# A two-layer decoder trunk with routed experts: three kept weight chunks instead of one, a ring of eight instead of twelve, and VectorE's waits for itself moved

## What is computed

```python
def peer_ffn(h, w_q, sub_keys, expert_u, expert_v):      # per block of 128 rows
    q = jnp.einsum('nd,de->ne', xb, w_q).reshape(n, 8, 2, 128)
    s = jnp.einsum('nhie,ike->nhik', q, keys)
    top_s, top_i = lax.top_k(s, 16)                      # per head and half
    cand_s = top_s[:, :, 0, :, None] + top_s[:, :, 1, None, :]
    best_s, best_pos = lax.top_k(cand_s.reshape(n, 8, 256), 16)
    idx = ...                                            # 8 heads x 16 experts of 16384
    gate = jax.nn.softmax(best_s, axis=-1)
    act = jax.nn.gelu(jnp.einsum('nhkd,nd->nhk', expert_u[idx], xb))
    return jnp.einsum('nhk,nhkd->nd', gate * act, expert_v[idx])
```

## Time and profile before

| | before |
|---|---|
| median of 3 runs | 1624.89 us (1624.58 to 1625.01) |
| the profiled execution, its own time | 1618.27 us |
| its span | 1616.2 us |
| TensorE matmul busy | 1189.6 us, 74% of the span |
| VectorE busy | 1149.4 us, 71% |
| ScalarE busy | 651.6 us, 40% |
| DMA moved | 665.08 MB |

### The profile page before, as it was taken

The page is one execution under the profiler, slowest core; times in us unless marked ns, Lnnn a source line. Parts: engine busy times, 40 slices in busy tenths (PEclk is TensorE's granted clock), DMA queues, the critical chain, the costliest instruction groups (busy, mean ns, idle before and its releaser), DMA issues.

```text
span 1616.2 us, 22343 instructions
## 1 busy us (share of the span) xinstructions
PE 1189.6 (74%) x7488; PEld 589.1 (36%) x7488; DVE 1149.4 (71%) x3098; ACT 651.6 (40%) x1743; POOL 600.5 (37%) x542
## 2 busy tenths in 40 slices
PE   8977776777649986968786788789697955555546
PEld 3662232234316662422263356444234611111111
DVE  4498768568687687776677867779855876666654
ACT  0233255233336664653233466556322333333332
POOL 1036334434324343324333424432342344444441
PEclk9999998989879998989898899899898978777787
DMA  9899999999999999999999999999999999999995
GB/s 373 352 368 418 422 422 421 422 422 421 423 421 421 423 420 422 421 423 422 423 422 422 396 424 424 420 422 419 402 425 422 419 422 421 421 421 421 420 420 236
DMA packets 84371, 665.08 MB, mean 412 GB/s; under 512 B 9408, under 2 KB 9680, under 8 KB 11424
## 3 DMA queue, kind: packets, MB, share of 16 engines
q0 software_dynamic: 74752, 540.13, 80.7%
q1 hardware_dynamic: 9504, 123.53, 18.2%
HBM read 662.57 MB, written 1.05 MB: 411 GB/s over the span
## 4 chain that ended last, share of the span: by engine, by line
DMA 37%; PE 29%; DVE 21%; issue 6%; ACT 5%; POOL 1%; POOLq 0%; ACTq 0%; DVEq 0%; SPq 0%
DMA ring<-in_experts,idx 36%; PE acc L947 12%; DVE ring L1614 7%; PE act_bank L621 7%; PE dve_bank L607 5%; PE act_bank L854 2%; DVE onehot L1245 2%; POOL ring L511 1%; ACT diag L1175 1%; DVE scratch L1245 1%; PE act_bank L607 1%; ACT h L1086 1%; DVE h L1409 1%; DVE picked L1571 1%; ACT scratch L1006 1%
## 5 line engine op out<-in xcount | busy, mean ns | idle before, releaser
L511 POOL DMA_INDIRECT ring<-in_experts,idx x510 | 573.5, 1125 | 936.5 <-PE acc L947 742.3
L1614 DVE CUSTOM_DVE_ANT_0 ring<-ring,hn 128x1024 f32<-128x1024 f32 x512 | 625.9, 1235 | 322.4 <-DMA ring<-in_experts,idx 309.6
L947 PE MATMUL acc<-ring,diag 64*64 64x512 f32 x4080 | 598.5, 711 | 327.8 <-ACT diag L1175 303.1
L947 PEld LDWEIGHTS acc<-ring,diag 64*64 64x64 f32 x4080 | 153.8, 152 | 677.6 <-ACT diag L1175 427.7
L1006 ACT ACTIVATE acts<-dots 128x2 f32<-128x2 f32 x256 | 52.1, 204 | 764.2 <-DVE dots L1614 763.5
L621 PE MATMUL act_bank<-hnT,wbuf 128*128 128x128 f32 x1728 | 221.1, 287 | 25.5 <-ACT h L1086 20.5
L621 PEld LDWEIGHTS act_bank<-hnT,wbuf 128*128 128x128 f32 x1728 | 208.2, 199 | 71.3 <-issue 62.9
L1006 ACT ACT_TABLE_LOAD x148 | 189.9, 1283 | 13.0 <-DVEq L367 2.2
L1175 ACT ACTIVATE diag<-cst,coefs 128x64 f32<-128x64 f32 x512 | 150.2, 340 | 10.2 <-PE acc L947 1.9
L1166 ACT ACTIVATE coefs<-acts,gate 128x1 f32<-128x1 f32 x512 | 122.8, 286 | 12.1 <-ACT scratch L1006 0.8
L1006 ACT ACTIVATE scratch<-act_bank 128x512 f32<-128x512 f32 (+3 forms) x73 | 35.7, 489 | 73.5 <-PE act_bank L621 62.9
(11 more groups left out here) (173 smaller groups left out, 996.2 us busy)
## 6 DMA issues: line engine op xcount, KB each, us to landing
wbuf<-in_weights SPq DMA_DIRECT2D x48, 2048.0 KB, 12.4
ring<-in_weights SPq DMA_DIRECT2D x7, 2048.0 KB, 20.2
ring<-in_experts,idx POOLq DMA_INDIRECT x510, 22.5
kept<-in_weights SPq DMA_DIRECT2D x2, 2048.0 KB, 22.2
wbuf<-in_weights SPq DMA_DIRECT2D x2, 512.0 KB, 6.3
wbuf<-in_weights SPq DMA_DIRECT2D x1, 1024.0 KB, 8.7
scratch<-in_bias POOLq DMA_DIRECT2D x1, 1024.0 KB, 11.9
scratch<-in_bands POOLq DMA_DIRECT2D x1, 768.0 KB, 13.5
```

The lines of the kernel that those rows point to most:

```text
L511: pool.indirect_dma_start(ring[:, n % RING], None, io[f"experts{layer}"], bass.IndirectOffsetOnAxis(idx[:, at:at + 1], 0),).then_inc(sem(f ...
L947: last[rows] = pe.matmul(acc[rows][half][home:home + HALF_P], diag[part, n % DIAGS], ring[part, slot, D + half * CW:D + (half + 1) * CW], ...
L1614: dve.tensor_tensor_reduce(out=ring[:, slot, 0:D], in0=ring[:, slot, 0:D], in1=hn[:, phase % NBLK], scale=1.0, scalar=0.0, op0=ALU.mult, o ...
```

## The change

Five things are altered. RING goes from 12 to 8. KEPT goes from one to three chunks per layer: chunks 7, 8 and 9 of layer 0, chunks 13, 15 and 11 of layer 1; the two query chunks 8 and 9 of the first block no longer lie in the ring, and STAGED_AT places five chunks in four. ASKED_FIRST goes from 2 to 10, and the top-16 searches of heads 6 and 7 of the first block from slots 4 and 5 to slots 8 and 12. VectorE's lane gets `run`, which starts an instruction and leaves its wait `pending` until the next instruction of the lane; a dot between the two is started without it. `copy_even` lets its copies themselves raise `even_copied`.

```diff
-RING = 12
+RING = 8
-STAGED_AT = (5, 3, 0, 1, 2, 4, 5)
+STAGED_AT = (3, 2, 0, 1, 3)
-KEPT = ((7,), (13,))
+KEPT = ((7, 8, 9), (13, 15, 11))
-ASKED_FIRST, QUERIED_BY = 2, 14
+ASKED_FIRST, QUERIED_BY = 10, 14
-TOPS_DUE = [-3, -2, 0, 1, 2, 3, 4, 5]
+TOPS_DUE = [-3, -2, 0, 1, 2, 3, 8, 12]
...
+            def settle(self):
+
+                if self.pending:
+                    self.after(self.pending)
+                    self.pending = None
+
+            def run(self, operation, *operands, name=None, **more):
+
+                self.settle()
+                self.pending = self.start(operation(*operands, **more), name)
...
             def tt(out, in0, in1, op=ALU.mult, name=None):
-                lane(dve.tensor_tensor(out, in0, in1, op), name)
+                lane.run(dve.tensor_tensor, out, in0, in1, op, name=name)
...
-                lane.after(started[-1])
+                lane.pending = started[-1]
...
             def copy_even(phase):
 
+                lane.settle()
                 for rows in range(2):
                     dve.wait_ge(sem(f"pairs_summed{rows}"), (phase + 1) * STEPS * GROUPS + AHEAD)
...
-                        started = lane.start(dve.tensor_copy(h[part, phase % NBLK, cols], acc[rows][half][part]))
-                    lane.after(started)
-                    lane.tell("even_copied")
+                        started = lane.start(dve.tensor_copy(h[part, phase % NBLK, cols], acc[rows][half][part]),
+                                             "even_copied" if rows else None)
+                    lane.pending = started
```

More of the change, by code:

```diff
@@ L350, in __init__ @@
             def __init__(self, eng, own):
-                self.eng, self.own, self.count, self.seen = eng, own, {}, {}
+                self.eng, self.own, self.count, self.seen, self.pending = eng, own, {}, {}, None
             def start(self, instruction, name=None):
@@ L1270, in square_sum @@
             def square_sum(b, out):
-                lane(dve.tensor_tensor_reduce(out=out, in0=h[:, b], in1=h[:, b], scale=1.0, scalar=0.0,
-                                              op0=ALU.mult, op1=ALU.add, accum_out=stat[:, 0:1]))
+                lane.run(dve.tensor_tensor_reduce, out=out, in0=h[:, b], in1=h[:, b], scale=1.0, scalar=0.0,
+                                              op0=ALU.mult, op1=ALU.add, accum_out=stat[:, 0:1])
             def row_root():
@@ L1339, in bias_scores @@
                     top = stat[:, 64:64 + n]
-                    lane(dve.reduce_max(top, part, AX))
+                    lane.run(dve.reduce_max, top, part, AX)
                     tt(part, part, top.unsqueeze(2).to_broadcast([P, n, keys]), ALU.subtract, "scores_biased")
@@ L1357, in mixer0 @@
                     part = probs[:, i % 2].rearrange("p (j k) -> p j k", k=keys)
-                    lane(dve.reduce_sum(total, part, AX))
-                    lane(dve.reciprocal(total, total))
+                    lane.run(dve.reduce_sum, total, part, AX)
+                    lane.run(dve.reciprocal, total, total)
                     tt(part, part, total.unsqueeze(2).to_broadcast([P, n, keys]), name="probs_ready")
@@ L1558, in expert_numbers @@
                     lane.after(started[1])
-                    lane(dve.tensor_copy(place, pos_lo[:, picks]))
+                    lane.run(dve.tensor_copy, place, pos_lo[:, picks])
                     stt(beyond, row, float(WHOLE), place, ALU.is_ge, ALU.mult)
+                    lane.settle()
                     lane.start(dve.tensor_tensor(row, row, beyond, ALU.add))
@@ L1650, in last_rows @@
                     home = slice(half * HALF_P, (half + 1) * HALF_P)
-                    lane(dve.tensor_copy(h[0:HALF_P, NBLK - 1, half * CW:(half + 1) * CW], acc[0][half][home]))
+                    lane.run(dve.tensor_copy, h[0:HALF_P, NBLK - 1, half * CW:(half + 1) * CW], acc[0][half][home])
+                    lane.settle()
                     lane.tell("last_rows_ready0")
@@ L1657, in experts @@
                     g = first + n // BODY
+                    if n == 0:
+                        lane.settle()
                     dot(phase, g, n % BODY)
```

47 lines of the change are left out of this document (30 added, 17 removed).

## The result

| | before | after |
|---|---|---|
| median | 1624.91 us, 4 runs (1624.58 to 1625.01) | 1648.86 us, 4 runs (1640.79 to 1655.09) |
| ratio | | 1.0145 (1.01 to 1.019) |
| the profiled execution, its own time | 1618.27 us | 1640.79 us |
| its span | 1616.2 us | 1639.0 us |
| DMA moved | 665.08 MB | 656.69 MB |

The change is slower by 1.45%, 24 us, where 5 us less was forecast; the time lies far outside 1609 to 1630. In two later series it was slower by 1.17% and 1.26% (e8, e13). The runs of the changed kernel lie 14 us apart, those of the kernel before 0.4.

What follows compares the result with a forecast made beforehand. DMA was taken to bound the kernel. Bytes -19.9, standstills +19.1, VectorE's waits -4.4 and the start +0.2 gave -5.0 us, from 1624.89 to 1619.9 us, range 1609 to 1630.

Steps and rivals of the forecast that it cites:

- Bytes: Four second-block chunk loads (8, 9 of layer 0; 11, 15 of layer 1) go: -19.9 us, nothing hidden.
- nor around the other removed loads: Outside the fifth place, no removed load has a room (gather m's landing minus issue of m + 4) short.
- the fifth place: Mixer 1, gather 340: short by 1.6 us plus 5.0 for the spared load issued at 1126.85, 6.6 in all.
- five places: Bursts at gathers 62, 142, 192, 268, 340 with rooms under 5.7 us: standstills 2.7, 4.4, 2.2, 3.2, 6.6, sum +19.1.
- a standstill shifts everything behind it, so that only the largest of a burst counts: Within one burst of side work neighbours' shortfalls do not add; only the largest is priced.
- m = 192: Gather 192, in one burst of side work: room 3.5 us against 5.7 needed, short by 2.2.
- VectorE's waits: 203 dots no longer wait for VectorE itself, about 0.1 us each; in the bursts -4.4 us (nothing to -6.6).
- first rival: The moved waits are worth nothing, as the skill page says: +0.6 us, 1625.5 us, no change; chance 20%.
- The start: First sums and gathers 8 to 16, moved heads answering the shallow ring: +0.2 us (3 less to 4 more).
- From there I let them land every 2.5 us: After gather 12 lands at 121.2 us, landings every 2.5 us put gather 16 at 131.2, against 131.0 before.
- second rival: Each standstill slows the next two sums (1.2 GHz clock): 3.5 us per place, +12.4, 1637; chance 22%, at about 1629.
- Its milder form: Standing still slows one sum at each of the five places: +3.7 us in all, 1628.6 us.

Runs made afterwards that it cites:

- e8: The changed kernel itself run again on another chip, nothing altered; ratio to the kernel before 1.0117.
- e13: The changed kernel again, as baseline on one chip with e14 and e16; 1644.51 us, ratio to the kernel before 1.0126.
- e5: The kernel before (12 slots) with the four second-block chunk loads cut to 64 KB each, leaving stale weights; ratio to the kernel before 0.9894.
- e14: The changed kernel with only layer 0's chunks 8 and 9 spared, layer 1's 11 and 15 loaded again; 1649.83 us, ratio to before 1.015.
- e4: The changed kernel with all four spared chunks loaded again for the second blocks (bytes of before, 8 slots); ratio to the kernel before 1.0195.
- e16: The same kernel as e4, run on the chip of e13; 1654.53 us, ratio to the kernel before 1.018.
- e7: The changed kernel with 10 slots, the loads of before and heads 6 and 7 ahead as before; ratio to the kernel before 1.0022.
- e1: The kernel before (12 slots, one kept chunk, old head order) with only VectorE's waits moved; ratio to the kernel before 0.9991.
- e2: The changed kernel with VectorE's waits as they were before; ratio to the kernel before 1.0161.
- e3: The changed kernel with heads 6 and 7 ahead of the first sums as before; ratio to the kernel before 1.0165.
- e11: The changed kernel with 10 slots and two kept chunks per layer, waits and heads moved; ratio to the kernel before 0.9926.
- e17: The same kernel as e11, run again beside e18 on one chip; 1612.42 us, ratio to the kernel before 0.9923.
- e9: The kernel before, 12 slots and its bytes kept, gathers issued only 8 slots ahead of the sums; ratio to the kernel before 1.0222.
- e18: The kernel of e17 with heads 6 and 7 ahead of the first sums as before; 1618.76 us, ratio to the kernel before 0.996.

## Why the prediction was wrong, step by step

**The bound was right.** DMA is it, and e5 shows that with 12 slots bytes are time: 17 us for 19.

**Bytes: counted in full, half came back.** The step that failed is "nor around the other removed loads". There I took the rooms from the trace of before as they were, with the loads still in the queues. But a load that goes takes its 5.0 us away from every gather behind it, as I had reckoned at the fifth place alone. Ahead of gather 122 one load is missing; what is behind could land 5.0 us earlier, the sums were not ready for it, and DMA stood still there for 3.4 to 4.6 (changed kernel, e8, e13, e14; nothing in e4 and e16). The fifth place itself came out about as reckoned: its dips, gathers 335 to 349, lose 0.7 us in e4, which has the load, and 5.8 in the changed kernel and in e8 (6.6 forecast). The two places together are nearly all that was lost of the saving. Measured for all four loads: 10.0 us left of 19.9 (e13 to e16), where I had 14.9.

**Rooms: five places at 19.1 us, measured 37 to 42.** With the bytes of before, the ring of 8 with moved waits and heads costs 32 us (e4); by my terms it would be 14.1 (the list without the 5.0 of the spared load) + 0.2 - 4.4 = 9.9. Two steps failed. The first: "a standstill shifts everything behind it, so that only the largest of a burst counts". The view of DMA from 640 to 672 us, 40 slices of 0.8 us, changed kernel:

```profile
DMA  9999996598999993106689898996999999999997
GB/s 420 420 430 399 430 420 256 205 215 287 399 410 399 348 389 133 51 31 102 184 338 461 348 369 369 389 184 266 420 389 451 399 420 379 348 399 389 389 369 317
DMA packets 1461, 10.66 MB, mean 333 GB/s; under 512 B 161, under 2 KB 161, under 8 KB 161
```

This is the burst around my place m = 192, priced at 2.2 us (gather 192 itself goes at 671.1, and one more dip of 1.3 us is there). The mean of 333 over 32 us is (421 - 333) / 421 x 32 = 6.7 us, most of it in three dips. So one standstill does not buy the burst out. I read it so: the engines stay late by the same work, each late sum sends the gather eight slots on late too, and the ring comes round again (eight slots are 19.9 us) while the burst lasts. That reading is argued; the dips are measured.

Over the whole trace, between 135 and 1580 us, I count stretches below 85% of 421 GB/s in which over 0.3 us is lost: 4 in the kernel before (3 us), 33 in the changed one (40 us), 41 in e8 (45 us), 32 in e4 (33 us) and 10 in e7 (8 us); I had five. e4, with the bytes of before, shows where the terms went wrong. The largest dip of each place is about what I had priced: 2.0 us at gather 63 (2.7), 4.1 at 141 (4.4), 2.3 at 187 (2.2), 3.2 at 269 (3.2), 0.4 at 341 (1.6), in all 12.0 against 14.1. But further dips in the same bursts add 9.8 us, which I had struck out as bought, and dips elsewhere 10.8. All short rooms of the trace before from gather 60 on, neighbours included, sum to 41.8 us: too much against these 33, but nearer than 14.1.

The second: I asked when the last of the 16 DMA engines had landed a gather, and counted a room as sufficient from 5.7 us on. At 7 of the 10.8 us elsewhere (gathers 161, 219, 245, 289, 313, 390) the trace before has no room under 5.7. Either the rate falls already with a room just above it, or lateness was carried there; no run parts the two, and which of the two steps weighs more stays open.

What would have shown it: the loop played as a loop. I did it afterwards with numbers of the trace of before alone: each pair's lag from its landing to its sum as it was there (median 8.8 us, one in ten over 15.5), DMA at 421 GB/s and 3.2 us from issue to first bytes. It gives no standstill with 12 or 10 slots and 24 us with 8; with 2 us more of flight 0, 1.5 and 55. It is an estimate, and coarse (another way of taking the lags gives 44 in place of 24, and with 10 slots 5 us were measured), but it has the steepness that e7 and e4 show, and says slower.

**VectorE's waits: about right in size, near the noise.** The row at the same place now is

```profile
485.44 0.17 DVE L374 CAST idx<-pos_f 128x16 uint32<-128x16 f32 x1
485.53 1.22 DVE L1636 CUSTOM_DVE_ANT_0 ring<-ring,hn 128x1024 f32<-128x1024 f32 x1
```

The dot starts 0.08 us before the conversion ends, where it started 0.03 after the earlier trace rows: 0.11 us each, a little more than the 0.09. In time: e1, where the ring is deep, 1.5 us, hardly to be told from nothing; with 8 slots e2 lies 3 to 7 us above the three series of the changed kernel, against my 4.4, with 3 to 4 us of uncertainty and more against the first. So the first rival, and the rule of the page "VectorE: DVE Perf Modes" of the Trainium skill (section "The DRAIN you can't avoid") that semaphores between instructions cost nothing, do not describe these dots: the row shows them overlapping VectorE's own work, which they couldn't do behind a wait. The same section of the Trainium skill says that a next operation which is not held starts earlier, and with that the row agrees; its figure of eight copies is of another case than a dot behind a short conversion.

**The start: +0.2 forecast, about +6.** The first sum was right: 103.7 us in e8 (103.3 forecast), gather 8 at 104.67 (104.2). The second ended at 111.7 (110.2), for the larger part since it took 3.26 us, not 1.95: from 108.4 to 111.8 the granted clock was 0.59, so for most of it 1.2 GHz. The step that failed is "From there I let them land every 2.5 us". The diagonals of the fourth pair are written at 115.46, but its sum starts at 120.45, since TensorE has the four steps between ahead of it: the stream into `acc`, half of head 7's query, a wait for ScalarE, the keys. Gathers 14 and 15 go at 123.25 and after. It stood in the order that I had shown; I followed it for three sums and not for the fourth. From 80 to 135 us DMA moved 373 GB/s before and 327 in e8: 46 / 421 x 55 = 6.0 us. The moved heads are a gain all the same: e3, which differs from e8 by them alone and has no halt either, moved 290 GB/s there, 4.8 us worse than e8.

**The second rival had the sign and at most a part of the loss.** TensorE's time for all 4080 multiplications of the sums is 598.5 us before and 609.7 after.

```profile
L947 PE MATMUL acc<-ring,diag 64*64 64x512 f32 x4080 | 598.5, 711 | 327.8 <-ACT diag L1175 303.1
```

```profile
L958 PE MATMUL acc<-ring,diag 64*64 64x512 f32 x4080 | 609.7, 723 | 315.1 <-ACT diag L1186 291.2
```

At 1.74 us more for a slow sum (3.69 against 1.95) that is six slow ones more. Its milder form, one more at each of five places, is borne out in number, and it put the time at 1628.6. If each of the six held DMA up for its full 1.74 us, they would be 11 of the 37 to 42 us; how many did, no run shows. But e11 and e17 with ten slots have as many (608.7 and 609.1 us) and stand still only 6 us longer than before, so slow sums alone don't make the loss. My own margin was mis-reckoned beside it: the gain falls below 0.2% from 0.36 us more per place ((5.0 - 3.2) / 5), not from 0.7. The rule of the Trainium skill's page "DMA: Bandwidth & Descriptors" (section "Anatomy of one DMA — SWDGE (gpsimd) path"), by which each place would have been 1.3 us less short, pointed the wrong way: the loss was larger than with 5.7, not smaller, and the shortest flight in any of the traces is 5.3 us (e4).

**Together.** 32 us for the ring (e4), less the 10 to 13 that the spared loads give, is 19 to 22; measured were 19 to 24.

## What to carry to other kernels

The price of a shallower ring is not read off as the sum of a few shortfalls in the trace of the deep one: late sums come in bursts longer than the ring, each short gather of a burst costs again, and the loss is small down to some depth and steep below it (here 5 us, then 28). So take half the step first: 10 slots and two kept chunks win 6 us, with the moved heads 12 to 13, where 8 and three lose 19 to 24. Where bytes are taken out of a queue that is also the cover for late work, reckon everything behind them earlier, at each place. And when work is put behind the first sums, follow the order until the queue is full again, not for the first sum alone.

## What was unexpected of the hardware

The halt. TensorE ends head 3's query at about 86 us and goes on at 92, ScalarE with it, while VectorE and POOL work on; no other instruction, landing or load of the trace stands behind it. The semaphore that ScalarE waits for is the one which this query's last multiplication raises: it comes at 92.32, where that multiplication, whose end is modelled, should end at 86.48 (in e8 at 85.65, and the semaphore at 85.67). It is in the traces of the changed kernel and of e9 to e18, eleven of eleven, whatever the ring, the waits or the order, and in none of e1 to e8. The kernel before took 1619.3 and 1619.9 us in the series of e1 to e8, and 1624.9 to 1625.6 in the others: by about the 6 us of the halt. The given trace of before, 6.6 us under the median of its runs, has none either. So it looks like something of a chip (the series on 6 and 1 have it, those on 9 and 12 do not), which one execution can escape; its cause is open. It means that the profiled executions of before and after in the first series differ in more than the change, and that ratios are best compared among series of one kind.

With the shallow ring the time may be looser too: the runs of the changed kernel lie 14, 4 and 7 us apart in its three series, those of the kernel before 0.4, 5 and 2.
